# Mixer, routing and last expert of a two-block kernel in another order

## The reference

```python
def first_block(...):
    for l in range(DEPTH):                       # DEPTH = 2
        h = x * (1.0 + sc_m) + sh_m
        mix = token_mixers(h, ...)               # attention, retention, mLSTM, then w_out
        x = layer_norm(DEEPNORM_ALPHA * x + (1.0 + g_m) * mix, ...)
        h = x * (1.0 + sc_f) + sh_f
        y = moe_ffn(h, ...)                      # all 16 experts, gate 0 where not routed
        x = layer_norm(DEEPNORM_ALPHA * x + (1.0 + g_f) * y, ...)
```

## Time and profile before

| what | us |
|---|---|
| runs of the kernel | 1797.24, 1804.73, 1805.1; median 1804.73 |
| the profiled execution's own time | 1802.9 |
| its span | 1801.1 |
| TensorE busy in it | 1660.1 |
| its mean granted TensorE clock | 0.963 of full |

### The profile page before, as it was taken

How to read it: one execution, slowest core, us unless ns; L and a number is a source line. 1 busy time by engine, 2 the same in 40 slices (tenths; PEclk the granted TensorE clock), 3 DMA queues, 4 the chain that set the end, 5 groups by cost and what they waited for, 6 DMA issues and landing times.

```text
span 1801.1 us, 19027 instructions
## 1 busy us (share of the span) xinstructions
PE 1660.1 (92%) x7427; PEld 1252.3 (70%) x7427; DVE 1086.8 (60%) x1659; ACT 723.6 (40%) x1093; POOL 0.2 (0%) x4
## 2 busy tenths in 40 slices
PE   2999989999998989899999959899999898999998
PEld 2555557888884545577888848778887677778885
DVE  7587478777655753785454465774454647754446
ACT  0123334343421233333343336664344656544345
POOL 0000000000000000000000000000000000000000
PEclk9999999999999989999999979899999999899999
DMA  8755444786764623347455626144455442336551
GB/s 318 247 192 212 157 171 173 260 308 235 266 217 152 218 86 117 110 153 261 157 196 192 209 76 186 48 141 140 164 187 214 167 142 94 112 100 209 180 182 47
DMA packets 218458, 314.98 MB, mean 175 GB/s; under 512 B 22388, under 2 KB 147708, under 8 KB 218240
## 3 DMA queue, kind: packets, MB, share of 16 engines
q1 hardware_dynamic: 218368, 313.76, 50.6%
HBM read 312.70 MB, written 1.05 MB: 174 GB/s over the span
## 4 chain that ended last, share of the span: by engine, by line
PE 83%; DVE 9%; ACT 4%; issue 3%; SPq 0%; DMA 0%; DVEq 0%; ACTq 0%
PE psum L543 18%; PE psum L544 18%; PE psum L545 18%; PE psum L509 10%; PE psum L902 3%; DVE gring_parts L1193 2%; PE psum L550 2%; DVE tmp L1196 1%; PE psum L586 1%; PE psum L1080 1%; PE psum L529 1%; PE psum L531 1%; PE psum L530 1%; ACT arena L2159 1%; PE psum L773 1%
## 5 line engine op out<-in xcount | busy, mean ns | idle before, releaser
L545 PE MATMUL psum<-arena_parts,hT_parts 128*128 128x512 f32 x960 | 381.0, 397 | 0.0
L1193 DVE TENSOR_TENSOR gring_parts<-gring,arena_parts 128x2048 fp32r<-128x2048 f32 x120 | 269.7, 2288 | 54.8 <-ACT arena_parts L2159 54.7
L1193 DVE TENSOR_TENSOR arena_parts<-psum,ex_parts 128x256 fp32r<-128x256 f32 x108 | 45.4, 420 | 301.5 <-ACT ex_parts L2159 301.5
L2159 ACT ACTIVATE arena_parts<-gring 128x2048 fp32r<-128x2048 f32 x120 | 223.6, 1916 | 0.4
L544 PE MATMUL psum<-gring_parts,arena_parts 128*128 128x512 f32 x544 | 219.2, 403 | 0.0
L545 PEld LDWEIGHTS psum<-arena_parts,hT_parts 128*128 128x128 f32 x960 | 182.1, 190 | 43.1
L2159 ACT ACTIVATE ex_parts<-psum 128x256 fp32r<-128x256 f32 x108 | 41.2, 382 | 417.9 <-PE psum L586 417.9
L509 PE MATMUL psum<-gring,hT 128*128 128x512 f32 (+1 forms) x448 | 203.5, 609 | 5.3 <-DVE hT L1190 3.7
L543 PE MATMUL psum<-arena_parts,o_cat_parts 128*128 128x512 f32 x512 | 205.5, 401 | 0.0
L544 PE MATMUL psum<-gring_parts,o_cat_parts 128*128 128x512 f32 x512 | 203.7, 398 | 0.0
L543 PE MATMUL psum<-arena_parts 128*128 128x512 f32 x448 | 178.5, 398 | 5.8 <-DVE gring_parts L1193 5.8
(11 more groups left out here) (229 smaller groups left out, 2256.0 us busy)
## 6 DMA issues: line engine op xcount, KB each, us to landing
gring<-in_w_ada SPq DMA_DIRECT2D x24, 2048.0 KB, 9.8
gring<-in_w_ffn_in SPq DMA_DIRECT2D x44, 1024.0 KB, 8.5
gring<-in_w_in SPq DMA_DIRECT2D x16, 2048.0 KB, 12.4
gring<-in_w_gate SPq DMA_DIRECT2D x32, 1024.0 KB, 7.4
gring<-in_w_up SPq DMA_DIRECT2D x32, 1024.0 KB, 9.8
dring<-in_w_down SPq DMA_DIRECT2D x32, 1024.0 KB, 5.0
dring<-in_w_ffn_out SPq DMA_DIRECT2D x22, 1024.0 KB, 5.0
gring<-in_w_out SPq DMA_DIRECT2D x8, 2048.0 KB, 7.9
```

What stands on the lines that cost most here:

```text
L545: return nc.tensor.matmul(ps, lo, w, start=False, stop=stop)
L1193: return nc.vector.tensor_tensor(o, a, b, op)
L2159: return nc.scalar.activation(o, a, ACT.Copy)
```

## The change

**TensorE, attention loop.** `between(s)` stands between the transposes and the values of step s, and holds one half projection in each of the eight steps. `mqk(1)` and two column sums go ahead of the loop, the sum for chunk 7 goes from step 3 to step 5 and to bank 6, `ml_scores(0)` ahead of the last half, `ml_scores(1)` behind the first half of `rvg`. **VectorE** takes `att_in(s + 2)` first in a step, `gate_sums` in step 1, chunk 7 in step 2. **ScalarE** does the softplus before the first exponential and `att_probs_T` and `att_exp` first in each step. The mLSTM normalisation of both tiles becomes one set of instructions; `root_of("ret")` goes behind `copied_oT(3)`. **Experts:** six of the eight k of `gu(1, 0)` run before `tr(0, 0)`, into bank 6. The tail becomes `tr(15,0) gu(15,1) dn(15,0) tr(15,1) dn(14,1) dn(15,1)`. **Second block:** half 0 of `avcv` is rounded during expert 15, into half of an expert buffer; half 1 is rounded earlier on ScalarE; VectorE interleaves the residual of tile 1 with the norm of tile 0.

```diff
-        def rounded(name, q):
-
+        def rounded(stage, name, q):
+
+            if (stage, name, q) == (SECOND[0], "avcv", 0):
+                return w_hi[0][:, 4:8, :]
             if name in IN_DOWN:
                 return dring_rest[:, q].rearrange("p f (h n) -> p (f h) n", n=N)
             return w_hi[name != "pg1"][:, 4 * q:4 * q + 4, :]
...
-                return (FIRST[-1], T, ("dn1", NE - 2 + q)) if stage == SECOND[0] else (SECOND[0], T, ("e", 1, 1))
+                return (FIRST[-1], T, ("dn1", NE - 1) if q else ("gu1", NE - 2)) if stage == SECOND[0] else (SECOND[0], T, ("e", 1, 1))
...
+        used[0] = free
+        last_hidT, last_hidT_lo = buf(FE // P, P, of=arena_parts), buf(FE // P, P, of=arena_parts)
...
+        def hid_T(stage, e, t):
+
+            if (stage[0], e, t) == ("a", NE - 1, 1):
+                return last_hidT, last_hidT_lo
+            return hidT[:, t], hidT_lo[:, t]
+
+        def gu_bank(stage, e, t):
+
+            return 6 if (stage[0], e, t) == ("a", 1, 0) else t
...
+            first = stage[0] == "a"
+            if first:
+                gu(1, 0, range(6))
             tr(0, 0)
-            gu(1, 0)
+            gu(1, 0, range(6 if first else 0, KT))
             tr(0, 1)
             dn(0, 0)
-            for e in range(1, ne):
+            for e in range(1, ne - first):
                 gu(e, 1)
                 tr(e, 0)
                 dn(e - 1, 1)
@@ -609,6 +628,12 @@
                 tr(e, 1)
                 sums(e)
                 dn(e, 0)
+            if first:
+                tr(ne - 1, 0)
+                gu(ne - 1, 1)
+                dn(ne - 1, 0)
+                tr(ne - 1, 1)
+                dn(ne - 2, 1)
             dn(ne - 1, 1)
...
-                    take(("ml", "O", 0), V, 7)
+                    take(("ml", "O", 0), V, 6)
                     pe.sem_inc(waited)
-                    take(("ml", "O", 1), V, 6)
+                    take(("ml", "O", 1), V, 7)
...
-                if s == 0:
-                    mqk(1)
-                    mix_sum(4, 6)
-                    mix_sum(5, 7)
-                if s == 1:
-                    half_in_proj("mvo", 0, 0)
-                    half_in_proj("mvo", 0, 1)
+                if s < 4:
+                    half_in_proj("mvo", s // 2, s % 2)
                 if s == 2:
                     if l == 0:
                         mix_sum(6, 7)
-                    half_in_proj("mvo", 1, 0)
-                if s == 3:
-                    if l == 0:
-                        mix_sum(7, 7)
-                    half_in_proj("mvo", 1, 1)
                 if s == 4:
                     half_in_proj("rqk", 0, 0)
                 if s == 5:
                     gate_columns()
                     half_in_proj("rqk", 0, 1)
+                    if l == 0:
+                        mix_sum(7, 6)
                 if s == 6:
                     half_in_proj("rqk", 1, 0)
                     if l == 0:
                         mix_sum(8, 6)
                 if s == 7:
+                    ml_scores(0)
                     half_in_proj("rqk", 1, 1)
                     if l == 0:
                         mix_sum(9, 6)
-                    ml_scores(0)
 
             att_scores(0)
             att_scores(1)
+            mqk(1)
+            mix_sum(4, 6)
+            mix_sum(5, 7)
             for s in range(len(ATT)):
-                between(s)
                 if s + 2 < len(ATT):
                     att_scores(s + 2)
                 att_transposed(s)
+                between(s)
                 att_values(s)
-            ml_scores(1)
             for h in range(NR):
                 half_in_proj("rvg", h // 2, h % 2)
+                if h == 0:
+                    ml_scores(1)
...
+            if gated:
+                gated_hid(ne - 1, 0)
+                down_rest(ne - 1)
+                hid_rest(ne - 1, 0)
+                more(ne - 1)
+                gated_hid(ne - 1, 1)
+                hid_rest(ne - 1, 1)
...
             for s in range(len(ATT)):
+                if s + 2 < len(ATT):
+                    att_in(s + 2)
                 if s == 0:
                     sum_gate(4, bank(V, ("sum", "ada4")), "ada4", 2 * l + 1)
                     sum_gate(5, bank(V, ("sum", "ada5")), "ada5", 2 * l + 1)
                     ada_of(6)
                 if s == 1:
-                    ada_of(7)
+                    gate_sums()
                 if s in (1, 2) and l:
                     dve.wait_ge(rows_loaded, rows_count(FIRST[l - 1]))
                     gain_and_bias(s - 1, ("affine", "in", s - 1))
                 if s == 2:
+                    ada_of(7)
                     columns_of(6)
-                    gate_sums()
...
-                    columns_of(7)
                     ada_of(8)
...
                     rope_chunk("rqk", 0, 2 * NR)
+                    columns_of(7)
...
-                if s + 2 < len(ATT):
-                    att_in(s + 2)
...
             for h in range(NR):
-                if h + 1 < NR:
+                if 0 < h < NR - 1:
                     ml_args(h + 1)
                 ml_weights(h)
+                if h == 0:
+                    ml_args(1)
 
             ret_weights(0)
             ret_weights(1)
             dve.wait_ge(tensor_done, T.at(V, ("ml", "PV", NR - 1)))
-            for t in range(TT):
...
+                if (l, e) == (DEPTH - 1, NE - 1):
+                    chunk_rest(SECOND[0], "avcv", 0)
...
             if l == 0:
-                chunk_rest(stage, "avcv", 0)
-                joined(0)
+                for h in range(2):
+                    joined(0, h)
+                moments("in", 0)
                 scaled(0)
-                joined(1)
-                pre_norm("mix", 0)
-                scaled(1)
+                joined(1, 0)
+                pre_var("mix", 0)
+                joined(1, 1)
+                pre_scaled("mix", 0)
+                moments("in", 1)
                 modulated("xT", "hT", 0, g_mix)
                 features_rest("hT", 0, h_hi[1])
+                scaled(1)
                 chunk_rest(stage, "avcv", 1)
                 pre_norm("mix", 1)
...
             copied_mqk(0)
+            act.wait_ge(vector_done, V.at(A, "negabs"))
+            activate(grow[0:NR, 5, :], grow[0:NR, 5, :], ACT.Exp).then_inc(scalar_done, A.step())
+            act.wait_ge(scalar_done, A.now())
+            activate(grow[0:NR, 5, :], grow[0:NR, 5, :], ACT.Ln, bias=ones[0:NR, 0:1]).then_inc(scalar_done, A.step("softplus"))
+            act.wait_ge(scalar_done, A.now())
             att_exp(0)
             att_exp(1)
+            copied_mqk(1)
             for s in range(len(ATT)):
-                if s == 0:
-                    copied_mqk(1)
+                att_probs_T(s)
+                if s + 2 < len(ATT):
+                    att_exp(s + 2)
                 if s == 1:
                     copied_mvo(0)
-                    act.wait_ge(vector_done, V.at(A, "negabs"))
-                    activate(grow[0:NR, 5, :], grow[0:NR, 5, :], ACT.Exp).then_inc(scalar_done, A.step())
-                    act.wait_ge(scalar_done, A.now())
-                    activate(grow[0:NR, 5, :], grow[0:NR, 5, :], ACT.Ln, bias=ones[0:NR, 0:1]).then_inc(scalar_done, A.step("softplus"))
-                    act.wait_ge(scalar_done, A.now())
...
             root_of("ml", hv)
-            root_of("ret", ret_hv)
             rounded_weights(0, range(1, 2))
             copied_oT(3)
+            root_of("ret", ret_hv)
             copied_oT(2)
...
                 table_of(ACT.Sqrt)
-                rounded_half(stage, "avcv", 0)
                 root_of("in", rstd[:, 0:1], 0)
+                rounded_half(stage, "avcv", 1)
                 act.wait_ge(vector_done, V.at(A, ("x", "in", 0)))
-                sum_squares(("pre", "mix"), 0, x, arena[:, 2 * KT * N:2 * KT * N + D])
+                sum_squares(("pre", "mix"), 0, x, arena[:, KT * N:KT * N + D])
+                modulated_T("xT", "hT", 0, g_mix, hi=h_hi[1])
                 root_of("in", rstd[:, 1:2], 1)
-                rounded_half(stage, "avcv", 1)
-                modulated_T("xT", "hT", 0, g_mix, hi=h_hi[1])
                 act.wait_ge(vector_done, V.at(A, ("x", "in", 1)))
```

More of the change, by code:

```diff
@@ L403, in program @@
         acc = tmp
+        free = used[0]
         sT = buf(2, 384)
@@ L2204, in act_experts @@
+            for e in range(ne - first):
+                silu(e, 0)
                 if following <= e + 1 < ne:
                     rounded_weights(e + 1, range(e == 0, 2))
-                act.wait_ge(DN.sem(A.stage, f"dn{e}"), DN.level(A.stage, f"dn{e}"))
-                copy(d_hi[e % 2], dslot(A.stage, f"dn{e}")).then_inc(scalar_done, A.step(("d_hi", e)))
-                act.wait_ge(tensor_done, T.at(A, ("gu1", e)))
-                activate(sact[:, 1, :], psum[:, 1, 0:FE], ACT.Silu, **scaled(1)).then_inc(scalar_done, A.step(("silu", e, 1)))
```

164 lines of the change are left out of this document (91 added, 73 removed).

## The result

| | before | after |
|---|---|---|
| median of the runs (us) | 1804.05 (1797.24 to 1805.10) | 1747.26 (1745.40 to 1747.96) |
| profiled execution, its span (us) | 1802.9, 1801.1 | 1747.96, 1746.2 |
| TensorE busy (us), mean clock | 1660.1, 0.963 | 1636.7, 0.978 |

The ratio is 0.9691 (95% interval 0.9666 to 0.9717): 3.1% faster. The forecast was 1755, range 1745 to 1775. By the profiled executions the change gives 54.9 us where the sum said 49.6. The one of before (1802.9) lies above most of its runs: three later sets of before have medians of 1799.67, 1799.85 and 1795.01, and against the set that ran on the same chip as a second set of after (1747.33) the gain is 52.5 us.

What follows compares the result with a forecast made beforehand. TensorE was taken to bound the experts, and waits for other engines plus low clock the loops and four places. Terms 12 + 4 + 11.8 + 11.6 + 1.9 + 8.3 = 49.6 off 1802.9 gave 1753.3 profiled, median 1755, range 1745 to 1775.

Steps and rivals of the forecast that it cites:

- The step that was mis-sized: Second block behind its first transposes: only a wait of 3.44 us becoming 2.6 was counted.
- The loop of layer 1: Attention loop, layer 1: 4 us gained after 6.4 of new waits, bounds 0 and 9.7; VectorE can't end before 170.6.
- The loop of layer 2: Attention loop, layer 2: halves cover the waits for ScalarE's copies; 12 us gained, bounds 7 and 15.
- The root: Mixer output, root of "ret" moved: TensorE's 4.00 us wait becomes 0.6; 5.9 us a layer, 11.8 for both.
- Expert 1 ahead of routing: Routing: 18 matmuls of gu(1,0) fill TensorE's 3.91 us gap; 5.8 us a layer, 11.6 for both.
- The tail: Expert 15: the residual starts at 537.02 + 0.42 instead of 539.39; 1.9 us gained, bounds 0 and 2.
- The second block's start: Second block's entry: residual 5.1 us earlier, transposes 7.5 earlier; 8.3 us gained in all, bounds 5 and 8.5.
- The softplus: Moved ahead of the attention loop: cost nothing, cover 2.4 us; a drain per table load would make the sum 1.7 smaller.
- (a): Rival: waits change places in the loops and at the second block's entry; 35.3 us gained, 1769; chance 0.16.
- (b): Rival: the clock falls anyway; of 20 us credited to it, half staying gives 1765, all 1775; chance 0.15.
- (c): Rival: slower, the experts' pipeline loses its slack, priced at 2 us an expert; 1815; chance 0.04.
- (d): Rival: no effect, loops give back what the four places win, needing 36 us of new waits; chance 0.03.

Runs made afterwards that it cites:

- experiment 8: The kernel after with the last expert's tiles in the other experts' order on TensorE, VectorE and ScalarE, both layers; early rounding kept: 1750.55 us.
- experiment 9: The kernel after with the rounding of avcv half 0 back at the second block's start, its rest first in VectorE's queue: 1754.89 us.
- experiment 1: The kernel after with ScalarE's root of the retention variance back directly behind that of the mLSTM variance, both layers: 1759.54 us.
- experiment 7: The kernel after with the softplus back at step 1 and VectorE's gate sums back at the end of step 2: 1750.24 us.
- experiment 10: The kernel after with the mLSTM norm computed tile by tile again, ten small VectorE instructions instead of five, both layers: 1747.89 us.
- experiment 3: The kernel after with each step's half projection ahead of the transposes on TensorE, in the attention loops only: 1801.35 us.
- experiment 4: The kernel after with both attention loops as before on all three engines, softplus, ml_scores(1) and ml_args included; four other parts kept: 1763.78 us.
- experiment 5: The kernel after with VectorE taking the next scores (att_in of step s+2) last in each step, as before: 1760.40 us.
- experiment 6: The kernel after with the softplus and its table loads back at step 1, behind the copy of mvo(0), both layers: 1762.47 us.
- experiment 2: The kernel after with all of the second expert's first product behind the first expert's transposes again, bank 0, both layers: 1758.54 us.

## Why the prediction was right, and where it was off

**The step that was mis-sized** is the one that counted nothing behind the second block's start but 0.8 us: the stretch gave 4.01. It carries 3.2 of the 5.3 us by which the sum fell short. TensorE's idle time there fell by 1.0 us (the wait of 3.44 is 2.88); the matmuls are the same 3496 rows, and no edit explains why they took 3.0 us less. Windows from the first transposes to the end, of before, of experiment 8 and of experiment 9:

```profile
1054.16:1801.10 746.94, 699.36 (x3496) 569.67 (x3496) 427.13 (x591) 386.49 (x628) 0.00 (x0) 0.96 0.42 141
```

```profile
1007.25:1747.80 740.55, 693.91 (x3496) 565.68 (x3496) 428.74 (x595) 385.46 (x628) 0.00 (x0) 0.97 0.42 142
```

```profile
1008.72:1756.50 747.78, 701.88 (x3496) 572.68 (x3496) 428.77 (x595) 385.58 (x628) 0.00 (x0) 0.96 0.42 141
```

The same matmuls are busy 693.9 to 701.9 us; what differs is how many of them ran at 1.2 GHz. By the clock records of the traces TensorE's clock stood at 1.2 GHz in this stretch for 60.9 us in before, 53.4 in after, 47.6 in experiment 8 and 65.1 in experiment 9. Over all traces the stretch takes 740.5 to 747.8. Two traces of one kernel (after) give 742.93 and 742.72, but those of some other kernels agree as well: experiments 1, 7 and 10 lie at 742.6 to 742.7, experiments 3 to 6 at 745.1 to 745.7. After happened to lie 4.0 below before. That a kernel fixes the length isn't shown: all kernels but after were traced once, the runs of before spread over 19 us (1791.61 with a mean clock of 0.967 to 1810.63 with 0.959), and the four runs of experiment 2 over 10 us (1751.22 with 0.980 to 1761.18 with 0.971). The entry of layer 2 up to the scores spreads likewise, from 67.37 to 70.35 in the experiments (71.13 in before); it takes 67.4 in the four traces where the clock doesn't fall in it, with the softplus ahead of the loop (experiment 3) as without (experiments 4, 6 and 7). What decides it is open. The Trainium skill (TensorE: Matmul & The Clock Gate, Part 1) says that the window in which TensorE's activity is watched runs freely and isn't started anew by a kernel. In the two traces of after the clock falls at the same places within 0.15 us (first at 132.96 and 133.10), and no run here shows whether that is chance.

The remaining 2.5 us of what the median was off are no term of the sum. The forecast put the median 1.8 us above the profiled time; in after it lies 0.7 below. The bounds were added up wrongly too: their lowest sum is 26.6 and their highest 58.6, not 28 and 57. The stated range would hardly change by that.

**The loop of layer 1** gave 5.80 where the term was 4. The sum had 6.4 us of new waits; the rows show 5.05: 2.25 for `mvo(1,0)` (1.5 forecast), 1.13 for `erow` where I had `mix_sum(7)`, 1.67 for the rotation (2.8), none for `rqk(0,0)` (0.7). The limit that I named for VectorE, 170.6, was not reached: its work without a wait ends at 170.08, but the second rotation and the last output are still to come and end at 177.33, 3.0 us earlier than before. TensorE's waits in the stretch fell by 2.4 us, from 7.4 to 5.0, and its busy time by 3.4. I estimate that half of this is clock: a stretch of busy time at 1.2 GHz costs half of its length, and that half was 5.1 us before and 3.4 after. The other half is overlap, as a row shows its whole length only ahead of a wait. Before, the first transposes take 0.44 us and then TensorE waits; in after the half follows 0.28 us behind their start (120.93 and 121.21).

**The loop of layer 2** gave 12.27 for 12, with the parts a little otherwise: all waits in the stretch went from 7.6 to 3.4 us (4.2, where 5.9 was reckoned, since the rotation cost 2.27 and not 1.4, and `rqk(1,1)` another 0.76), and the busy time fell by 8.0, of which 6.3 is clock by the same estimate where 6.1 was reckoned; the other 1.7 is overlap again, which the sum did not hold.

**The root** (5.69 and 5.78 for 5.9 each) is shown by experiment 1. **Expert 1 ahead of routing** was credited 5.8 a layer; the stretches say 4.61 and 5.80, and the limit was the gate of tile 1, 0.72 us ahead of `tr(0,1)`, not the rest of `hidT(0,0)`. **The tail** measured 1.22 (2.5 in idle time) and 2.06 for 1.9 and 2.2. **The second block's start**: 13.37 for 13.3 in its stretch, with expert 1 in it. No run undoes the new order of residual and norm on VectorE. By the rows the transposes came 13.89 us behind the first residual before (1040.27, 1054.16) and come 11.55 behind it now, so 2.3 of the 7.5 us are put down to it without an experiment.

**The softplus** ahead of the loop cost nothing, as forecast, but "nothing" was half of the story. Here is ScalarE in layer 2 of after, ahead of the first exponentials, then TensorE's first transposes:

```profile
599.63 0.41 ACT L2201 ACTIVATE ex<-ex 4x256 f32<-4x256 f32 x1
600.07 1.28 ACT L2201 ACT_TABLE_LOAD   x1
601.36 0.51 ACT L2201 ACTIVATE ex<-ex,ones 4x256 f32<-4x256 f32 x1
...
607.62 0.44 PE L783 MATMUL psum<-cshared,arena 128*128 128x128 f32 x2
```

TensorE doesn't wait. Nor is there a drain: the load ends at 601.35 and the next instruction starts 0.01 behind, so the larger price per load that the Trainium skill gives (ScalarE: Activation LUTs, What ACT_TABLE_LOAD costs) does not appear here. But without this move, the gate sums, put at step 1, would have cost 10.7 us in the two loops (experiment 6), more than half of what the loops give; with both left in their old places, the loops are 1.1 us longer (experiment 7). The prediction took the edit for a neutral one because it asked only what it costs where it goes, and not what waits for it.

**The rivals.** (a) Waits did change places in layer 1, but for less than the old ones. (b) Clock: by the estimate of half of the busy time at 1.2 GHz, clock cost 51.5 us from the first scores on before and 31.1 after. That is 20.4 us less, but 3.3 of it lies in the second block, where none was credited; 17.1 of the 20 credited came. (c) and (d) are out: experts take 17 us, the loops give 18.

## What to carry to other kernels

Orders written by hand on several engines are one object: a half moved by one place on TensorE alone cost 54 us, an edit that looks neutral (the softplus) was what let another be free (the gate sums in step 1). Before moving a step, write down for each engine what stands first in its queue and which instruction of the moved step that head waits for; buffers that are written two steps ahead count. And where TensorE's clock falls in waits, compare stretch by stretch: an unchanged stretch of 743 us moved by up to 7 us between kernels, as much as a good edit gives.

## What the runs showed of the hardware that was not expected

TensorE's clock made stretches without an edit differ: 740.5 to 747.8 us for the same 3496 matmul rows, with 742.93 and 742.72 in two traces of one kernel. In the stretches of the two loops, TensorE's waits fell by 6.6 us and its busy time by 11.5. The clock stood at 1.2 GHz for 27.3 us of them before and for 10.2 after, so it can have given at most 8.5 of the 11.5; about 8.1 is the estimate. The other 3.4 is what small matmuls no longer show when the next row follows at once. Filling 6.6 us of waits gave 18.1 us in all.
